# Expert weights loaded as plain 128-row blocks instead of as rows grouped by partition

## What is computed

```python
logits = (hf @ router_w + router_b)              # hf: 256 x 1024, 32 experts
top_logits, top_idx = lax.top_k(logits, 4)
gates = softmax(top_logits)
...
def expert_block(args):                          # the rows xb of one expert e
    gu = xb @ w_gate_up[e] + b_gate_up[e]        # w_gate_up[e]: 1024 x 2048
    gate = minimum(gu[..., :1024], 7.0)
    up = clip(gu[..., 1024:], -7.0, 7.0)
    act = (up + 1.0) * gate * sigmoid(1.702 * gate)
    return act @ w_down[e] + b_down[e]           # w_down[e]: 1024 x 1024
...
y = zeros.at[row_tok].add(y_rows * row_gate)     # weighted sum back to the tokens
```

## Time and profile before

| | us |
|---|---|
| three runs | 1259.65, 1262.73, 1263.48 |
| median | 1262.73 |
| the profiled execution, its own time | 1259.65 |
| its span in the profile | 1257.9 |
| PE busy | 1127.2 |
| DVE busy | 362.6 |
| ACT busy | 160.1 |

### The profile page before, as it was taken

One profiled execution on the slowest core, in us unless ns is written; L12 is line 12 of the kernel. 1 busy time (PEld: TensorE's weight loads), 2 busy tenths in 40 slices (PEclk: granted clock), 3 DMA queues, 4 the chain that ended last, 5 costly groups with the idle time before them and its releaser, 6 DMA issues.

```text
span 1257.9 us, 15864 instructions
## 1 busy us (share of the span) xinstructions
PE 1127.2 (90%) x6688; PEld 556.9 (44%) x6688; DVE 362.6 (29%) x713; ACT 160.1 (13%) x241; POOL 5.5 (0%) x23
## 2 busy tenths in 40 slices
PE   7999998888899999898989898999989898989895
PEld 6889987475433333332423333333323232333331
DVE  5582234244321321221221312212122121221312
ACT  3431133243000000100000000000010000000001
POOL 1000000000000000000000000000000000000000
PEclk9999998998899999999999999999999999999998
DMA  9731221465588999999999999999999999999994
GB/s 336 268 134 68 67 68 67 110 261 207 219 356 359 427 429 427 429 429 428 429 427 429 429 428 429 427 430 428 428 429 427 430 428 428 430 427 430 428 428 188
DMA packets 45159, 435.43 MB, mean 346 GB/s; under 512 B 6581, under 2 KB 6666, under 8 KB 20458
## 3 DMA queue, kind: packets, MB, share of 16 engines
q1 hardware_dynamic: 42986, 433.16, 82.6%
q10 hardware_dynamic: 2144, 1.86, 0.7%
HBM read 433.95 MB, written 1.05 MB: 346 GB/s over the span
## 4 chain that ended last, share of the span: by engine, by line
PE 64%; DMA 27%; DVE 5%; ACT 2%; issue 1%; SPq 0%; ACTq 0%; DVEq 0%
PE ps L1558 28%; DMA ring<-in_w_down 25%; PE ps L1585 7%; PE ps L1623 5%; PE ps L1244 4%; PE ps L1200 4%; PE ps L1537 4%; PE ps L1300 3%; PE ps L1296 2%; PE ps L1182 2%; DVE work L1125 2%; PE ps L1429 1%; PE ps L1473 1%; DMA work<-in_b_down 1%; DMA ring<-in_w_in 1%
## 5 line engine op out<-in xcount | busy, mean ns | idle before, releaser
L1558 PE MATMUL ps<-ring,work 128*64 128x512 f32 x2016 | 445.4, 595 | 22.3 <-DMA ring<-in_w_gate_up 20.8
L1558 PEld LDWEIGHTS ps<-ring,work 128*64 128x64 f32 x2016 | 141.9, 137 | 302.2 <-issue 258.9
L1585 PE MATMUL ps<-ring,work 128*64 128x512 f32 x1008 | 229.1, 598 | 42.5 <-ACT work L623 23.6
L1585 PEld LDWEIGHTS ps<-ring,work 128*64 128x64 f32 x1008 | 68.3, 136 | 181.6 <-issue 113.4
L1102 DVE TENSOR_SCALAR work<-ps 128x512 f32<-128x512 f32 x32 | 21.9, 686 | 212.9 <-PE ps L1182 212.9
L621 ACT ACTIVATE work<-work 128x512 f32<-128x512 f32 x32 | 20.2, 630 | 488.7 <-DVE work L1102 488.7
L1125 DVE COPY work<-ps 128x1024 f32<-128x1024 f32 x16 | 19.6, 1224 | 217.6 <-PE ps L1591 217.6
L1623 PE MATMUL ps<-work 128*128 128x512 f32 x128 | 59.2, 605 | 21.1 <-DVE work L1125 21.1
L1117 DVE COPY work<-ps 128x512 f32<-128x512 f32 x16 | 11.1, 691 | 229.8 <-PE ps L1182 229.8
L1182 PE MATMUL ps<-small,work 128*128 128x128 f32 (+1 forms) x353 | 57.6, 297 | 13.6 <-DMA work<-in_gdn_conv_w 6.4
L623 ACT COPY work<-ps 128x512 f32<-128x512 f32 x32 | 18.7, 585 | 363.1 <-PE ps L1182 363.1
(11 more groups left out here) (209 smaller groups left out, 665.6 us busy)
## 6 DMA issues: line engine op xcount, KB each, us to landing
ring<-in_w_gate_up SPq DMA_DIRECT2D x126, 2048.0 KB, 24.8
ring<-in_w_down SPq DMA_DIRECT2D x63, 2048.0 KB, 22.9
ring<-in_w_in SPq DMA_DIRECT2D x7, 2048.0 KB, 16.0
ring<-in_xattn_w_kv SPq DMA_DIRECT2D x2, 2048.0 KB, 14.5
ring<-in_w_out SPq DMA_DIRECT2D x2, 2048.0 KB, 8.4
work<-in_w_gate_up SPq DMA_DIRECT2D x2, 2048.0 KB, 12.8
ring<-in_xattn_w_q SPq DMA_DIRECT2D x1, 2048.0 KB, 9.4
ring<-in_xattn_w_o SPq DMA_DIRECT2D x1, 2048.0 KB, 8.9
```

Of the source, the lines that this page charges most:

```text
L1558: last = nc.tensor.matmul(bank(b)[p], xg_T[k][:, kb, :], w[:, kk, 512 * q:512 * q + 512], start=(kb == 0), stop=False)
L1585: last = nc.tensor.matmul(bank(Y_BANK + y)[p], act_T[:, b, HALF * c:HALF * c + HALF], w[:, b, 512 * q:512 * q + 512], start=(c == 0 and b ...
```

## The change

The chunks are loaded in plain blocks of 128 rows: in a chunk of w_gate_up, partition p holds the rows p and 128 + p of the 256; in a chunk of w_down the rows p, 128 + p, 256 + p and 384 + p of the 512. The chunks, their size, order and slots stay. With the plain order, `gather` and `act_turned` read contiguous columns, and DVE takes the gain from `cols`; the tile `ffn_gain`, its load on ACT's queue and DVE's wait for it are dropped.

```diff
-        ffn_gain = tiny(KB)
...
-                gu = [w_gate_up[0, bass.ds(2 * i + k, 1)].rearrange("e (c p j) n -> p (e c) (j n)", p=P, j=2)
-                      for k in range(2)]
-                dn = [w_down[0, bass.ds(2 * i + k, 1)].rearrange("e (c p j) n -> p (e c) (j n)", p=P, j=4)
-                      for k in range(2)]
+                gu = [w_gate_up[0, bass.ds(2 * i + k, 1)].rearrange("e (k p) n -> p (e k) n", p=P) for k in range(2)]
+                dn = [w_down[0, bass.ds(2 * i + k, 1)].rearrange("e (k p) n -> p (e k) n", p=P) for k in range(2)]
...
-                        src = gu[c // 4][:, c % 4, :]
+                        src = gu[c // 4][:, 2 * (c % 4):2 * (c % 4) + 2, :]
...
-                        src = dn[(c - 8) // 2][:, c % 2, :]
+                        src = dn[(c - 8) // 2][:, 4 * (c % 2):4 * (c % 2) + 4, :]
...
-                    sp.dma_start(dst, src).then_inc(S(loaded), 16)
+                    sp.dma_start(dst.rearrange("p (k n) -> p k n", n=src.shape[2]), src).then_inc(S(loaded), 16)
...
-            act.dma_start(ffn_gain.rearrange("p (c j) -> p c j", j=2),
-                          norm_ffn_g[0].rearrange("(c p j) -> p c j", p=P, j=2)).then_inc(S("ffn_gain_loaded"), 16)
...
-            v.wait_ge(S("ffn_gain_loaded"), 16)
...
-                                        spread(ffn_gain, SLOTS), ALU.mult) \
+                                        spread(cols[:, ROWS["ffn"]:ROWS["ffn"] + KB], SLOTS), ALU.mult) \
...
-                                                    split[s][:, t, 2 * P * (b // 2) + b % 2:2 * P * (b // 2 + 1):2],
-                                                    pick[k][:, t, :],
+                                                    split[s][:, t, b * P:(b + 1) * P], pick[k][:, t, :],
...
-                    last = turn("", bank(ACT_T_BANK[k])[:, P * b:P * b + P], up_sb[:, b:512:4])
+                    last = turn("", bank(ACT_T_BANK[k])[:, P * b:P * b + P], up_sb[:, P * b:P * b + P])
```

## The result

The changed kernel takes 1285.65 us (median of four runs, 1284.39 to 1286.59), the kernel before 1261.60 us (median of four: the three runs of the table ahead and one of 1260.47 us). The ratio is 1.0186, with a 95% interval of 1.0172 to 1.0200, or 24 us more. The prediction was 1284 us, with a range of 1264 to 1289 us.

A forecast was written before the change was run, and what follows sets the result against it. The prediction took the expert stage to be bound by weight transfers. Profiled 1259.65 us + 21.7 us for extra packets - 0.2 us for other edits gave 1281.2 us; 3.1 us more for the median gave 1284 us, range 1264 to 1289 us.

The forecast's parts named there:

- What bounds the kernel: Expert stage: weight transfers set the pace at 58.76 us a pair of experts, with some 4 us of PE slack.
- The price of a packet: Expert weight loads: 9.4 ns for each extra packet, 160 a pair on each engine, +1.50 us a pair.
- the bound from below: Expert weight loads: xattn_w_o's 422 GB/s with 4,096-byte rows gives 3.1 ns a packet, +7.2 us in all.
- Queued against standalone: Expert weight loads: packet price taken from queued loads, 9.4 ns, not from loads standing alone, 3.1 to 4.8 ns.
- standalone price: Rival, chance 0.22: expert loads pay only 3.1 to 4.8 ns a packet, +7 to +11 us, 1270 to 1274 us.
- The number of pairs: Expert stage: 14.5 pairs run at the transfers' pace, from 386 us to the last landing, together +21.7 us.
- Edits costed at nothing: Transposes, gather, gain multiply and dropped gain load: hidden in PE's slack or never late; only 0.2 us saved.
- Blocked issues: SP's load issues: may wait up to 7.4 us for queue room, behind some 20 us of queued transfers, costing nothing.
- No effect: Rival, chance 0.10: the packet price in the expert loads is hidden, 428 GB/s stays, 1262.5 us.
- faster: Rival, chance 0.06: shorter packets even out the engines in the expert loads, 435 GB/s, -13 us, 1250 us.
- Memory side: Rival, chance 0.07: a partition's weight rows 0.5 or 1 MiB apart in memory cost extra, over 1288 us.

The follow-up runs named there:

- e1: The changed kernel with the loads left in the grouped order of before (all edits but the loads): 1260.14 us, ratio 0.9994 to the kernel before.
- e2: The kernel before with only its loads changed to plain rows (8,192 and 4,096 bytes): 1283.10 us, ratio 1.0178.
- e3: The kernel before with plain rows only in w_down (four runs of 4,096 bytes) and the operands that belong to it: 1276.88 us, ratio 1.0124.
- e4: The kernel before with plain rows only in w_gate_up (two runs of 8,192 bytes) and the operands that belong to it: 1268.91 us, ratio 1.0060.
- e6: The kernel before with all chunks loaded in four runs of 4,096 bytes a partition: 1307.66 us, ratio 1.0363.
- e8: The kernel before with at most two chunks in the load queue, where there were five: 1262.89 us, ratio 1.0013.
- e9: The changed kernel with at most two chunks in the load queue: 1284.79 us, ratio 1.0181 to the kernel before.
- e5: The kernel before with w_down chunks in four runs of 4,096 bytes a partition, 8 KiB apart instead of 512 KiB: 1278.37 us, ratio 1.0116.
- e7: The kernel before with all chunks loaded in eight runs of 2,048 bytes a partition: 1360.62 us, ratio 1.0784.
- e10: The kernel before with gate-up chunks loaded two at a time from the second pair on, in runs of 32,768 bytes: 1261.06 us, ratio 0.9995.

## Why the prediction was right

**What bounds the kernel: right.** e1 takes PE work away and gains nothing; e2 touches only the loads and has the whole loss.

**The price of a packet: right, and shown over a range.** The line through the earlier trace rows gave 9.4 ns; the five kernels with shorter runs give 9.4 to 10.0 ns by the windows, and 9.4 to 9.5 ns where the landings are read. The predicted period was 60.25 us, the measured one 60.24 us. The prediction had only sizes of 16,384 and 2,048 bytes, and took those between from a straight line that e3, e4 and e6 bore out. The closeness of the total is in part luck: the difference forecast was 21.5 us (1284.2 - 1262.73), the measured one is 24.05 us, and the median that I started from was 1.1 us above that of the four runs. The rate of xattn_w_o in the earlier trace rows, the bound from below, would have given 7 us and was misleading: with 4,096-byte runs in all chunks (e6) the window has 410 GB/s, not 422. The 422 came from 2 us with 206 packets, some 13 on each engine.

**Queued against standalone: the right row for an unproven reason.** I chose the row in the queued state. e8 shows that a queue of two chunks costs what one of five does, and e9 shows the same at the sizes of the change. So what sets the standalone loads apart is not a depth beyond two. That they are one 2 MiB load and then nothing is what is left, but no run tries it, and why a packet seems cheaper there stays open. One argument of mine against the standalone price was weak: at 74.6 ns for 2,048 bytes, 612 ns leave some 15 ns for a packet of 16,384 bytes and 84.7 ns leave 10 ns for one of 2,048, so the two sizes don't give the one fixed part of 9 ns that I read from them.

**The number of pairs: nearly right.** 14.5 pairs at 1.51 us (60.24 - 58.73) are 21.9 us; the stage became 23.0 us longer. The last landing of the kernel after comes 61.84 us after that of the pair before it, where the period is 60.24 us. This excess of 1.6 us is 1.3 us more than in the kernel before (59.04 against 58.73 us), and it was not in the sum. e9 shows that SP's waits for room are not behind it. One other transfer falls into the last pair in every kernel, ACT's load of the final gain:

```profile
work<-in_final_norm_g ACTq DMA_DIRECT2D x1, 512.0 KB, 6.5
```

In the kernel after it is issued at 1259.88 us, 6.4 us ahead of the last landing at 1266.27 us. At the window's 418 GB/s its 0.52 MB take the engines 1.25 us, an estimate. The kernels whose w_down chunks have runs of 4,096 bytes show an excess of 0.9 to 1.6 us (1.0 in e2, with the same loads as after; 1.0 in e3, 0.9 in e5, 1.0 in e6), and 2.7 us in e9; before and e4, with 16,384 bytes there, show 0.3 us. So the excess goes with short runs at the end, and the load on ACT's queue is a candidate for the reason. Why it would cost less beside long packets is open, and no run moves it, so this is not shown.

**Edits costed at nothing: right.** Shorter transposes, the plain gather, the gain from another tile and the dropped load together have the ratio 0.9994, with an interval of 0.9981 to 1.0007 (e1). The sum had -0.2 us for them, too little to be told from nothing.

**Blocked issues: right.** They appeared, up to 6.0 us, and cost nothing (e9).

**The rivals.** Standalone price: it would have been 0.77 us a pair, measured 1.53 us. No effect and faster: excluded by the interval. Memory side: excluded for w_down by e5, and for w_gate_up by the even price, with rows 1 MiB apart in e4 and 16 KiB apart in e6. The Trainium skill (DMA: Bandwidth & Descriptors, Why small descriptors are slow) has about three cycles for a packet, by which the change would cost 8.2 us (an estimate from that page). The traces of e3 to e7 don't agree: they show some 9.5 ns, nearly three times the 3.5 ns of that estimate. The Trainium skill's figure of 512 bytes as the smallest transfer for line rate (the same page, Specifications) does not hold in this kernel's stream: 2,048 bytes give 387 GB/s, 4,096 give 410 and 16,384 give 429.

## What to carry to other kernels

When the DMA engines are the bound, count packets: each contiguous run on each engine costs a fixed 9 to 10 ns here beside its bytes (runs of 2,048 to 32,768 bytes), so take the layout in which a partition's bytes are one run, and let the other operand follow with a strided read, as the kernel before does. Price a stream from rows of a long stream, since short transfers standing alone ran 3 to 5% faster at the same size (422 against 410 GB/s with 4,096 bytes, 406 against 387 with 2,048), and such a row rests on 2 or 3 us. When transfers are made larger, look at both ends of the stream: e10 gained the rate and lost it again in the start-up and in the work left behind the last load.

## What was not expected of the hardware

Runs of 32,768 bytes are moved as single packets and still pay: 431 to 432 GB/s against 429 with 16,384 bytes. Reading the stationary operand of the gather (bfloat16) with a step of two columns costs nothing against contiguous ones, 2.80 us for 96 matmuls in both kernels; with a step of four, in e10, it takes 3.20 us:

```profile
376.42 3.20 PE ps L1552 x96
```

Contiguous columns made the four float32 transposes 0.1 us shorter than a step of four did (0.59 to 0.60 against 0.69 us), also with the loads as before (e1).
